# S5 branch output of a decoder step: from one piece and one PSUM bank to four pieces and two banks

## The reference, cut to what matters

```python
proj = h @ w_in                        # columns cut into qkv, z, a, b, u, gate_a, gate_b
ys, hr_new, hi_new = _s5(u, ...)       # linear state scan over 32 groups of 16 channels,
                                       # then y = C h + s5_d * u   (512 channels)
ys = jax.nn.gelu(ys).astype(x.dtype)
ys = ys * jax.nn.sigmoid(ys @ w_glu)   # w_glu: 512 x 512
y_b = ys @ w_b_up
```

## Time and profile before

| | us |
|---|---|
| median of 3 runs | 1792.56 (1790.83 to 1792.79) |
| the profiled execution, its own time | 1791.82 |
| its span in the trace | 1790.1 |
| PE busy over the span | 1516.5 (85%) |
| DVE busy | 699.3 (39%) |
| ACT busy | 410.1 (23%) |

### The profile page before, as it was taken

One profiled execution on the slowest core, in us unless ns is written; L12 is line 12 of the kernel. 1 busy time (PEld: TensorE's weight loads), 2 busy tenths in 40 slices (PEclk: granted clock), 3 DMA queues, 4 the chain that ended last, 5 costly groups with the idle time before them and its releaser, 6 DMA issues. The chain is left out here.

```text
span 1790.1 us, 15864 instructions
## 1 busy us (share of the span) xinstructions
PE 1516.5 (85%) x5982; PEld 942.4 (53%) x5982; DVE 699.3 (39%) x1073; ACT 410.1 (23%) x672; POOL 214.4 (12%) x222
## 2 busy tenths in 40 slices
PE   3999999828989889869988779999924999999970
PEld 3667665514666566535888646545422444444430
DVE  3594194411334433389478333322250111111117
ACT  6211200101647546322211410011100111111113
POOL 0000000000000000136248200000013000000004
PEclk9999999959999999989989989999956999999995
DMA  5135027051110110514210442211116999999947
GB/s 151 49 94 101 25 72 224 25 151 54 34 37 25 37 37 25 139 37 128 60 49 6 153 182 86 73 52 68 50 22 249 400 367 368 368 366 370 369 150 284
DMA packets 190883, 247.82 MB, mean 138 GB/s; under 512 B 62116, under 2 KB 125000, under 8 KB 190544
## 3 DMA queue, kind: packets, MB, share of 16 engines
q1 hardware_dynamic: 165176, 186.82, 32.8%
q10 hardware_dynamic: 18040, 34.45, 5.0%
q0 software_dynamic: 7584, 25.44, 3.8%
HBM read 188.86 MB, written 57.82 MB: 138 GB/s over the span
## 5 line engine op out<-in xcount | busy, mean ns | idle before, releaser
L650 PE MATMUL P<-arena 128*128 128x352 f32 (+1 forms) x1776 | 556.8, 470 | 0.0
L650 PEld LDWEIGHTS P<-arena 128*128 128x128 f32 (+1 forms) x1776 | 336.8, 193 | 191.4 <-issue 29.1
L1054 PE MATMUL P<-arena 128*128 128x512 f32 x512 | 226.7, 596 | 0.8 <-ACT arena L1993 0.8
L1054 PEld LDWEIGHTS P<-arena 128*128 128x128 f32 x512 | 95.4, 191 | 109.2 <-issue 109.2
L1002 PE MATMUL P<-arena 128*128 128x512 f32 (+1 forms) x288 | 126.8, 595 | 1.9 <-DVEq L1464 1.9
L970 PE MATMUL P<-arena 128*128 128x352 f32 x384 | 116.7, 468 | 10.2 <-DVE arena L1450 10.2
L1041 PE MATMUL P<-arena 128*128 128x512 f32 x256 | 115.3, 593 | 0.9 <-DVE arena L1593 0.9
L1573 DVE COPY arena<-P 128x512 f32<-128x512 f32 x32 | 22.1, 692 | 212.6 <-PE P L1028 212.6
L970 PEld LDWEIGHTS P<-arena 128*128 128x128 f32 x384 | 74.4, 194 | 52.9 <-issue 13.4
L1002 PEld LDWEIGHTS P<-arena 128*128 128x128 f32 (+1 forms) x288 | 50.9, 181 | 66.7 <-issue 64.2
L575 POOL TENSOR_TENSOR arena<-arena,N 64x256 f32<-64x256 f32 x96 | 79.6, 830 | 50.5 <-ACT arena L1927 26.9
(11 more groups left out here) (383 smaller groups left out, 1827.6 us busy)
## 6 DMA issues: line engine op xcount, KB each, us to landing
arena<-in_w_expert_up_dram SPq DMA_DIRECT2D x32, 2048.0 KB, 12.5
arena<-in_w_expert_down_dram SPq DMA_DIRECT2D x32, 1024.0 KB, 8.0
arena<-in_w_in_dram SPq DMA_DIRECT2D x36, 512.0 KB, 3.8
y_d<-arena ACTq DMA_DIRECT2D x32, 512.0 KB, 7.5
gate_d<-arena ACTq DMA_DIRECT2D x16, 528.0 KB, 4.1
arena<-gate_d SPq DMA_DIRECT2D x16, 528.0 KB, 4.5
arena<-in_x_prompt_dram SPq DMA_DIRECT2D x16, 512.0 KB, 4.2
y_d<-zero SPq DMA_DIRECT2D x1, 8192.0 KB, 33.7
```

Source lines behind the costliest of these rows:

```text
L650: m = pe.matmul(P[0:p, b + j, 0:TBK], w[:, k, 0:p], hT[:, k, TBK * j:TBK * j + TBK], start=f, stop=l)
L1054: m = pe.matmul(P[:, i % 2, :], xgT[i % 2][:, k, :], WU[i % NWE][:, k, :], start=k == 0, stop=k == KD - 1)
```

## The change

The 16 pairs alternate between bank 6 and bank 7. The output is handled in four pieces of eight groups (four pairs): the GELU, the stores and the reload of a piece are separate instructions, put among the later pairs on DVE, ACT and SP. `wglu` is loaded once `s_HB` is raised, ahead of the stores. The count of uses of bank 7 (`N7_Y`) is carried through. Since `U` and `Y5` are worked on in place, a piece's GELU writes only groups whose pairs have been made.

```diff
             def y_pair(a):
                 if a == 0:
                     pe.wait_ge(s_HB, 1)
-                o = bank6()[:, 0:2 * KS].rearrange("p (b k) -> p b k", b=2)
+                bank, s_b = (bank6(), s_6) if a % 2 == 0 else (bank7(), s_7)
+                o = bank[:, 0:2 * KS].rearrange("p (b k) -> p b k", b=2)
...
-                m.then_inc(s_6, 1)
+                m.then_inc(s_b, 1)
...
-            pe.wait_ge(s_ygT, 32)
+            pe.wait_ge(s_ygT, 16 * 5)
...
-            for a in range(GA):
-                bk = bank6()
+            def y_evict(a):
+                if a % 2 == 0:
+                    bk = bank6()
+                else:
+                    dve.wait_ge(s_7, N7_X + a // 2 + 1)
+                    bk = P[:, 7, :]
                 for b in range(2):
                     g = 2 * a + b
                     ins = dve.scalar_tensor_tensor(Y5[:, g, :], U[:, g, :], Dt[:, g:g + 1], bk[:, b * KS:(b + 1) * KS],
                                                    ALU.mult, ALU.add)
                     if b == 0:
                         link(ins)
-                read6(ins)
-            yf = Y5.rearrange("p a b -> p (a b)")
-            uf = U.rearrange("p a b -> p (a b)")
-            link(dve.tensor_tensor(uf, yf, yf, ALU.mult))
-            link(dve.tensor_scalar(uf, uf, 0.044715, 1.0, ALU.mult, ALU.add))
-            dve.tensor_tensor(uf, uf, yf, ALU.mult).then_inc(s_gl, 1)
-            dve.wait_ge(s_gla, 1)
-            link(dve.scalar_tensor_tensor(uf, uf, 1.0, yf, ALU.add, ALU.mult))
-            dve.tensor_scalar(yf, uf, 0.5, None, ALU.mult).then_inc(s_y5, 1)
+                if a % 2 == 0:
+                    read6(ins)
+                else:
+                    ins.then_inc(s_7f, 1)
+                    dve.wait_ge(s_7f, N7_X + a // 2 + 1)
+
+            def piece(t, j):
+                return t[:, 8 * j:8 * j + 8, :].rearrange("p a b -> p (a b)")
+
+            def gelu_in(j):
+                u, y = piece(U, j), piece(Y5, j)
+                link(dve.tensor_tensor(u, y, y, ALU.mult))
+                link(dve.tensor_scalar(u, u, 0.044715, 1.0, ALU.mult, ALU.add))
+                dve.tensor_tensor(u, u, y, ALU.mult).then_inc(s_gl, 1)
+
+            def gelu_out(j):
+                u, y = piece(U, j), piece(Y5, j)
+                dve.wait_ge(s_gla, j + 1)
+                link(dve.scalar_tensor_tensor(u, u, 1.0, y, ALU.add, ALU.mult))
+                dve.tensor_scalar(y, u, 0.5, None, ALU.mult).then_inc(s_y5, 1)
+
+            for j in range(4):
+                for a in range(4 * j, 4 * j + 4):
+                    y_evict(a)
+                    if a == 4 * j + 1 and j >= 1:
+                        gelu_out(j - 1)
+                gelu_in(j)
+            gelu_out(3)
...
-            for n in range(J_W + 2, J_Y + 1):
+            for n in range(J_W + 2, J_Y):
                 s5_job(n)
+
+            def tanh(j):
+                act.wait_ge(s_gl, j + 1)
+                u = U[:, 8 * j:8 * j + 8, :].rearrange("p a b -> p (a b)")
+                act.activation(u, u, ACT.Tanh, scale=0.7978845608028654).then_inc(s_gla, 1)
+
+            for j in range(3):
+                tanh(j)
+            s5_job(J_Y)
...
             act.sem_inc(s_fin, 2)
-            act.wait_ge(s_gl, 1)
-            uf = U.rearrange("p a b -> p (a b)")
-            act.activation(uf, uf, ACT.Tanh, scale=0.7978845608028654).then_inc(s_gla, 1)
+            tanh(3)
             for n in range(J_Y + 1, N_JOBS_S5):
                 s5_job(n)
...
-            sp.wait_ge(s_y5, 1)
-            for s in range(L):
-                sp.dma_start(yg_d.rearrange("g c s k -> s c g k")[s], Y5[s * GC:(s + 1) * GC]).then_inc(s_ygd, 16)
-            sp.wait_ge(s_ygd, 16 * L)
-            sp.dma_start(ygT, yg_d.rearrange("(j g) c s k -> (g c) j s k", g=8)).then_inc(s_ygT, 16)
+            sp.wait_ge(s_HB, 1)
             sp.dma_start(wglu, w_glu[0].rearrange("(k p) n -> p k n", p=128)).then_inc(s_ygT, 16)
+            for j in range(4):
+                sp.wait_ge(s_y5, j + 1)
+                g = slice(8 * j, 8 * j + 8)
+                for s in range(L):
+                    sp.dma_start(yg_d[g].rearrange("g c s k -> s c g k")[s],
+                                 Y5[s * GC:(s + 1) * GC, g]).then_inc(s_ygd, 16)
+                sp.wait_ge(s_ygd, 16 * L * (j + 1))
+                sp.dma_start(ygT[:, j], yg_d[g].rearrange("g c s k -> (g c) s k")).then_inc(s_ygT, 16)
```

More of the change, by code:

```diff
@@ L438, in hybrid_step @@
         N7_X = TT_ + 3 + 4 + L + 6
+        N7_Y = GA // 2
         N_CONST = 16
@@ L484, in KZ_COUNT @@
             return 2 * ((m - AB - 1) // 3) + (m - AB - 1) % 3
-        n7_scan = N7_X + 1 + 12 + sum({"q": 1 + 1, "k": 1 + 2 + 2 + 1, "v": 1 + 2 + 1}[k] for k, _ in
+        n7_scan = N7_X + N7_Y + 1 + 12 + sum({"q": 1 + 1, "k": 1 + 2 + 2 + 1, "v": 1 + 2 + 1}[k] for k, _ in
                                        JOBS[AB + 1:N_JOBS_QKV]) + 2 * HP
@@ L1760, in _ @@
                                      ACT.Copy))
-            for n in range(J_W + 2, J_Y + 1):
+            for n in range(J_W + 2, J_Y):
                 s5_job(n)
+            def tanh(j):
[5 more added lines that the diff above has]
+            s5_job(J_Y)
+            n7[0] += N7_Y
             bk = bank7()
```

## The result

The changed kernel takes **1749.28 us** (median of 4, 1746.94 to 1752.36) against 1792.67 for the kernel before (median of 4). The ratio is 0.9757, 95% interval 0.9742 to 0.9772. The forecast was 1747.4 us, a ratio of 0.975.

The account below looks back on a forecast made before the run. PE was taken as the bound, idle 36.6 us before the GLU behind a GELU, store, reload and `wglu` chain, and 7.2 us among pairs. 7.6 + 35.4 + 2.2 = 45.2 us less gave 1747.4 us, range 1744 to 1757.

Parts of the forecast that it names:

- The pairs, net 7.6: Job 14: with two banks steps fall from 7.07 to 6.00 us, saving 8.6 us, less 1.0 before the transposes.
- The added wait: Transposes of L770, which used a free bank 7, now wait for pair 15 to be read: 1.0 us lost.
- The cover of 2.8 us: Among the pairs: DVE's GELU work can grow 2.8 us a piece before PE stands waiting for a bank.
- The last piece: Behind the last pair: GELU 6.6, stores 5.6, reload 3.8 us; PE's gap before the GLU shrinks 36.6 to 1.2, saving 35.4.
- The clock, 2.2: First GLU group: with a gap of 1.2 us PE keeps the higher clock, saving 2.2 us; 7 us may lose it.
- What is moved and hidden: Pieces 0 to 2, `wglu` and later weight loads: SP needs about 6 us a piece, nothing paid until 12 us.
- Whole trip for the last piece (1): Last piece's store and reload cost 16.3 + 8.2 us whatever their size; 1764.5 us, chance 0.09.
- Stores that do not overlap (2): Each of a piece's eight stores pays 2.1 us landing, 16.8 in all, so pieces queue on SP; 1777.8 us, chance 0.05.
- DVE holding PE (3): Among the pairs GELU steps exceed the 2.8 us of cover; 8 us of stalls cancel the pairs' gain; 1755 us, chance 0.04.
- The price of the loads of `U` (4): A piece's stores cost as much as eight loads of `U`, 24.2 us, and queue on SP; 1807 us, chance 0.02.
- a later bound (5): Job 16 or what follows waits for something that does not move, so no net change; 1792 us, chance 0.02.

Follow-up runs that it names:

- two pieces: The changed kernel with the output handled in two pieces of eight pairs in place of four: 1761.96 us, ratio 0.9819.
- the kernel of one bank: The changed kernel with all pairs in bank 6 again, four pieces kept: 1760.41 us, ratio 0.9813.
- the kernel of eight pieces: The changed kernel with GELU and stores in eight pieces of two pairs, the reload still in four: 1748.60 us, ratio 0.9754.

## Why the prediction was right

**The pairs, net 7.6.** Measured 6.7 us (end of scan to transposes 54.9 before, 48.2 after). The term was mis-sized by 0.9. Some 0.7 of it is the step, 6.09 us and not 6.00, since the second pair's first matmuls take 0.73 us with no wait in front as well; I had put this down to the wait. The rest is the first step, which became only 0.91 us shorter, and 0.1 us at the transposes. The added wait is 1.00 as forecast. The edit alone moved the GLU by 8.0 us (7.6 over the stretch), as there the chain of DVE, which does not wait for the transposes, sets its start.

**The cover of 2.8 us.** Held: 2.6 us of further work a piece brought no wait, and 5.3 us moved pair 6 by 2.4, so the cover is 2.9. The forecast 0.2 us of lateness is there and costs nothing.

**The last piece.** GELU 6.6 forecast and measured; stores 5.6 forecast, 5.3 measured; reload 3.8 and 3.9. The wait came out at 0.9 for 1.2, so this term is 35.6 for 35.4. The bounds held, and two pieces showed that the price grows with size, but less than in proportion. The prediction had no row for pieces of this size and chose values inside wide bounds (4.1 to 7.1 and 2.05 to 8.2); that both came within 0.3 us is partly luck. That the 0.9 us of the pairs did not touch this term is not: it delayed job 15 and the data alike.

**The clock, 2.2.** The gain is there, 5.19 to 3.01. But the prediction spoke of losing it again only for a gap of 7 us, and far less was enough: 2.2 us in the kernel of one bank. A wait of 0.9 or 1.0 did not cost it in any of three profiles. Between 1.0 and 2.2 us nothing was run. The forecast had less room here than it said: its 1.2 us lie in that gap.

**What is moved and hidden.** One thing was overlooked and cost nothing: the issue of `wglu` held SP for 15.59 us, to 298.65, behind the zero fill. The first piece came at 302.6, so 4.0 us of cover. In the kernel of eight pieces, where DVE had the first piece ready at 293.5, its stores were issued only at 298.8.

**The sum.** 6.7 + 35.6 + 2.2 = 44.5, which is the whole difference of the stretch (147.66 - 103.12), against 45.2 forecast; nothing later gave it back (1359.3 and 1359.4 us). The medians differ by 43.4, and 1.1 us between that and the trace is within the spread of executions.

**The rivals.** Whole trip for the last piece (1): excluded by 5.3 us for its stores and 3.9 for its reload. Stores that do not overlap (2): each lands in 2.1 us, and eight are through in 5.3 and not 16.8, because they are issued 0.4 us apart. Here the Trainium skill's rule against transfers of this size ("DMA: Bandwidth & Descriptors", Bandwidth) does not decide: it is about bandwidth, four pieces moved the same bytes under the pairs, and the path paid for the last one alone. In bandwidth the traces agree with its direction: eight stores of 272 KB in 16.3 us are 137 GB/s, eight of 68 KB in 5.3 us are 105. DVE holding PE (3) is real from some 2.9 us of further work on. The price of the loads of `U` (4), 24.2 us, was not met, as the stores of a piece were through in 5.3 to 6.5; nor was a later bound (5).

## What to carry to other kernels

- Price a chain by its last piece and what covers it. Here three of four pieces of GELU, stores and reload went under the pairs, and job 15 covered nearly all of the fourth; the transfer named at the end of the wait (`wglu`) was worth 3 us of 36.6.
- When PE and its reader take turns on one PSUM bank, look at every such loop: the same edit was worth 7.6 us in the pairs, made alone, and 9.7 in the GLU.
- Waits of a microsecond and of two or three are not alike: behind the longer ones the clock can fall, and the matmuls that follow can pay more than the wait: some 5 us behind one of 2.2.

## What the runs showed of the hardware

- The granted clock fell to 0.50 (1.2 GHz) with waits of PE of 2.2, 3.6, 4.7, 6.1, 12.0 and 33 to 37 us before the GLU: during the wait where it was 3.6 us or more, and just behind it where it was 2.2. It cost 1.7 to 2.8 us there, and not the more the longer the wait: 2.8 us behind 3.6, 1.7 behind 6.1. It did not fall behind waits of 0.9 to 1.0. Of two equal waits of 2.22 us inside job 14 of one kernel, one was followed by the lower clock for some 10 us, the other not. What tells them apart stays open.
- The load of `wglu`, issued by SP 15.2 us after the 8 MB fill, stood 15.6 to 15.7 us in its issue in every kernel that had it there, and everything behind it on SP with it; issued after the reload it took 0.4 to 0.5. No run leaves the fill out, so that the fill is the reason is not shown.
- Eight stores of 68 KB, in rows of 544 bytes, are through in 5.3 to 6.5 us, eight of 136 KB in 9.1 and 9.6, eight of 272 KB in 16.3.
